# Value product by single heads with high and low parts side by side, and engine orders computed by a list scheduler

## The reference, cut to what matters

```python
s = jnp.einsum("bqhd,bkhd->bhqk", q, k) * scale      # 8 latent heads, then 8 sliding-window heads
s = jnp.where(mask, s, NEG)
p = jax.nn.softmax(s, axis=-1)
o = jnp.einsum("bhqk,bkhd->bqhd", p, v)              # the value product
```

## Time and profile before

| | |
|---|---|
| median of three runs | 1713.6 us |
| profiled execution | 1714.8 us, span 1713.1 us |
| TensorE (PE) busy | 1618.9 us, 95% |
| VectorE | 1127.7 us, 66% |
| GpSimd | 886.8 us, 52% |
| ScalarE | 778.4 us, 45% |
| mean granted TensorE clock | 0.97 of full speed |
| transfers | 285 MB, mean 167 GB/s |

### The profile page before, as it was taken

One profiled execution on the slowest core, in us unless ns is written; L12 is line 12 of the kernel. 1 busy time (PEld: TensorE's weight loads), 2 busy tenths in 40 slices (PEclk: granted clock), 3 DMA queues, 4 the chain that ended last, 5 costly groups with the idle time before them and its releaser, 6 DMA issues. The chain is left out here.

```text
span 1713.1 us, 29386 instructions
## 1 busy us (share of the span) xinstructions
PE 1618.9 (95%) x10253; PEld 1453.7 (85%) x10253; DVE 1127.7 (66%) x1953; ACT 778.4 (45%) x1628; POOL 886.8 (52%) x781
## 2 busy tenths in 40 slices
PE   7999988999997899999999879999999999999997
PEld 6788877888897789888878779999999999778876
DVE  6433344777675667676653696766776766799886
ACT  5221225666776666666542343333333333433354
POOL 1000002665654378686920488777777774444464
PEclk9999996999998999999989989999999999999999
DMA  8366653232322766655576436666666665965532
GB/s 279 117 200 225 219 170 103 59 105 66 84 69 52 199 178 169 176 160 155 168 237 187 157 100 189 179 181 198 205 190 194 189 195 164 355 228 172 177 119 92
DMA packets 218095, 285.35 MB, mean 167 GB/s; under 512 B 35929, under 2 KB 140506, under 8 KB 212780
## 3 DMA queue, kind: packets, MB, share of 16 engines
q1 hardware_dynamic: 217954, 283.53, 54.7%
HBM read 235.92 MB, written 114.67 MB: 205 GB/s over the span
## 5 line engine op out<-in xcount | busy, mean ns | idle before, releaser
L2488 POOL TENSOR_TENSOR lead<-acc,lead 128x512 fp32r<-128x512 f32 x110 | 148.6, 1359 | 104.5 <-ACT lead L2620 104.5
L1114 POOL TENSOR_SCALAR a_pr<-a_pr,a_rden 128x256 f32<-128x256 f32 (+7 forms) x128 | 94.1, 747 | 200.7 <-DVE a_rden L1214 195.9
L819 PE MATMUL zp<-win_h,xT_h 128*128 128x512 f32 (+1 forms) x288 | 113.1, 393 | 3.3 <-DVE acc L668 3.3
L819 PE MATMUL zp<-win_l,xT_h 128*128 128x512 f32 (+1 forms) x288 | 111.8, 388 | 0.0
L2620 ACT CAST lead<-acc 128x512 fp32r<-128x512 f32 x105 | 65.0, 620 | 100.3 <-PE z_ps L3146 58.1
L1155 ACT ACTIVATE a_pr<-a_pr,a_nm 128x256 f32<-128x256 f32 (+7 forms) x128 | 98.5, 772 | 22.3 <-DVE a_nm L1208 21.6
L2678 ACT CAST lead<-d_ring 128x512 fp32r<-128x512 f32 x73 | 45.4, 622 | 129.7 <-PE q_ps L3238 26.3
L1288 PE MATMUL a_o<-a_ph,a_vh 128*128 128x256 f32 x288 | 88.3, 306 | 12.7 <-DVE a_pl L1218 12.5
L819 PE MATMUL zp<-win_h,xT_l 128*128 128x512 f32 (+1 forms) x256 | 99.5, 389 | 0.0
L2559 POOL TENSOR_TENSOR u_op<-d_w,u_op 128x512 fp32r<-128x512 f32 x39 | 54.0, 1387 | 78.8 <-ACT u_op L2690 78.8
L2488 POOL TENSOR_TENSOR u_op<-acc,u_op 128x512 fp32r<-128x512 f32 x44 | 80.3, 1826 | 8.9 <-DVE o_tl L2836 8.9
(11 more groups left out here) (438 smaller groups left out, 5420.1 us busy)
## 6 DMA issues: line engine op xcount, KB each, us to landing
out_s_win_k<-in_state_win_k SPq DMA_DIRECT2D x40, 816.0 KB
out_s_win_v<-in_state_win_v SPq DMA_DIRECT2D x40, 816.0 KB
d_ring<-scratch_s_a SPq DMA_DIRECT2D x106, 256.0 KB, 3.3
acc<-in_state_win_k SPq DMA_DIRECT2D x16, 768.0 KB, 6.0
acc<-in_state_win_v SPq DMA_DIRECT2D x16, 768.0 KB, 5.5
scratch_s_a<-u_us SPq DMA_DIRECT2D x22, 544.0 KB, 6.1
acc<-in_w_gate SPq DMA_DIRECT2D x23, 512.0 KB, 8.9
acc<-in_w_up SPq DMA_DIRECT2D x22, 512.0 KB, 11.6
```

The lines of the kernel that those rows point to most:

```text
L819: last = nc.tensor.matmul(z[:, 0:n], a, b, start=(k == 0 and i == 0), stop=(k == KC - 1 and i == len(terms) - 1))
L1114: nc.gpsimd.tensor_scalar(p, p, self.rden[:, k % 2, h:h + 1], 1.0, ALU.mult, ALU.mult)\
L2488: nc.gpsimd.tensor_tensor(op[n][:, 1, :], src, op[n][:, 0, :].bitcast(F32), ALU.subtract).then_inc(S["lo"], 1)
```

## The change

The diff replaces how the value product is laid out, how its result leaves the bank, how banks are handed out, and how the orders are made.

**Value product.** `vh` and `vl` of a key block now lie in one tile `vv` of four groups of 64 columns: high 0, low 0, low 1, high 1. `ph` and `pl` lie in one tile `pp`, for each block and head the 128 high columns and then the 128 low ones. One matmul for each block and head takes 128 columns of `vv` (one head, high and low) against 256 columns of `pp` (the same head, high and low).

**Output.** In the bank, a head's own 64 rows hold high x high and high x low side by side, the other 64 rows hold low x high in the first 128 columns. VectorE adds the two halves with one `tensor_reduce` for each head, then ScalarE copies the cross terms to free columns of `pr`, then GpSimd adds them. The store waits for GpSimd.

```diff
-        self.vh = [sb(t(f"vh{i}"), [P, PT, 2 * HD], F32R) for i in range(2)]
-        self.vl = [sb(t(f"vl{i}"), [P, PT, 2 * HD], F32R) for i in range(2)]
-        self.ph, self.pl = (sb(t(n), [P, PT, 2, P], F32R) for n in ("ph", "pl"))
+        self.vv = [sb(t(f"vv{i}"), [P, PT, 4 * HD], F32R) for i in range(2)]
+        self.vh = [v[:].rearrange("p j (a c) -> p j a c", a=4)[:, :, 0:4:3] for v in self.vv]
+        self.vl = [v[:].rearrange("p j (a c) -> p j a c", a=4)[:, :, 1:3] for v in self.vv]
+        self.pp = sb(t("pp"), [P, PT, 2, 2, P], F32R)
+        self.ph, self.pl = (self.pp[:, :, :, i] for i in range(2))
+        self.cross = [self.pr[:, 0, i, SEQ - P:] for i in range(2)]
-        self.o_bank = ps(t("o"), [P, 2, P])
+        self.o_bank = ps(t("o"), [P, 2, 2 * P])
...
-            E.append((("value", k), 0.36 * (s + 1)))
+            E.append((("value", k), 0.24 * (s + 1)))
...
         elif what == "store":
-            sp.wait_ge(S["o_a"], n * PT + 4 * f + 4)
-            sp.wait_ge(S["o_d"], n * PT + 4 * f + 4)
+            sp.wait_ge(S["o_sum"], n * PT + 4 * f + 4)
...
     def gpsimd(self, pool, e):
+            v = self.vn[:].rearrange("p j (a c) -> p j a c", a=2)
+            nc.gpsimd.tensor_scalar(vh, v, 1.0, 1.0, ALU.mult, ALU.mult).then_inc(S["v_hi"], 1)
+            nc.gpsimd.tensor_tensor(vl, v, vh.bitcast(F32), ALU.subtract).then_inc(S["v_lo"], 1)
+        elif e[0] == "out":
+            pool.wait_ge(S["o_a"], 2 * k + 2)
+            pool.wait_ge(S["o_d"], 2 * k + 2)
+            nc.gpsimd.tensor_tensor(out, out, self.cross[k % 2], ALU.add).then_inc(S["o_sum"], 1)
...
     def scalar(self, act, e):
-            if s % 4 == 0 and n:
-                act.wait_ge(S[f"o_out{s // 4}"], 16 * n)
-            nc.scalar.copy(self.ot[0:HD, s * P:(s + 1) * P], self.o_bank[0:HD, 0, :]).then_inc(S["o_a"], 1)
+            act.wait_ge(S["o_d"], 2 * k + 2)
+            if k >= 2:
+                act.wait_ge(S["o_sum"], k - 1)
+            for h in range(2):
+                to, of = (slice(x * HD, (x + 1) * HD) for x in (h, 1 - h))
+                nc.scalar.copy(self.cross[k % 2][to], self.o_bank[of, h, 0:P]).then_inc(S["o_a"], 1)
...
     def vector(self, dve, e):
-            nc.vector.tensor_copy(self.ot[HD:P, s * P:(s + 1) * P], self.o_bank[HD:P, 1, :]).then_inc(S["o_d"], 1)
+            for h in range(2):
+                r = slice(h * HD, (h + 1) * HD)
+                nc.vector.tensor_reduce(self.ot[r, s * P:(s + 1) * P], self.o_bank[r, h].rearrange("p (a q) -> p q a", a=2),
+                                        AX.X, ALU.add).then_inc(S["o_d"], 1)
...
     def tensor(self, pe, e):
             if k:
-                pe.wait_ge(S["o_a"], k)
-                pe.wait_ge(S["o_d"], k)
+                pe.wait_ge(S["o_a"], 2 * k)
+                pe.wait_ge(S["o_d"], 2 * k)
-                    for i, (x, y) in enumerate(((vh, self.ph), (vh, self.pl), (vl, self.ph))):
-                        last = nc.tensor.matmul(self.o_bank[:], x[:, kb, :], y[:, kb], start=(kb == 0 and i == 0),
-                                                stop=(kb == s and i == 2))
+                    for h in range(2):
+                        last = nc.tensor.matmul(self.o_bank[:, h], self.vv[n % 2][:, kb, h * P:(h + 1) * P],
+                                                self.pp[:, kb, h].rearrange("p a q -> p (a q)"),
+                                                start=(kb == 0 and h == 0), stop=(kb == s), skip_group_check=True)
```

```diff
+        for u, (e, _) in enumerate(used["tensor"]):
+            self.use[e], self.at[e] = u, placed[e]
+            self.prior[e], holder[placed[e]] = holder[placed[e]], e
...
     def take(self, pe, e):
-        u = self.use[e]
-        if u >= len(self.banks):
-            self.done(pe, self.by[u - len(self.banks)])
+        if self.prior[e]:
+            self.done(pe, self.prior[e])
         return self.bank(e)
...
+    def start(self, part):
+        needs = [(x, lag) for x, lag in self.needs[part] if x in self.busy]
+        if any(x not in self.end for x, _ in needs) or any(x in self.busy and x not in self.end for x in self.gate.get(part, ())):
+            return None
+        at = max([self.clock[part[1]]] + [self.end[x] + HAND[part[1]] + lag for x, lag in needs])
+        if part in self.gate:
+            banks = self.free_banks()
+            return max(at, banks[0][0]) if banks else None
+        return at
...
+    def step(self):
+        best = None
+        for eng in ENGINES:
+            able = []
+            for i in range(2):
+                kinds = set()
+                for x in self.waiting[eng, i]:
+                    if x[1][0] not in kinds:
+                        kinds.add(x[1][0])
+                        at = self.start((i, eng, x[1]))
+                        if at is not None:
+                            able.append((at, x))
+                    if len(kinds) == AHEAD:
+                        break
+            if able:
+                until = max(self.clock[eng], min(at for at, _ in able)) + SLACK
+                at, x = min((c for c in able if c[0] <= until), key=lambda c: self.place[c[1]])
+                if best is None or at < best[0]:
+                    best = at, eng, x
+        at, eng, (i, e) = best
+        if part in self.gate:
+            self.placed[e] = self.free_banks()[0][1]
...
-            run(own, ring, sides, turns_of(weave(sides, ((0, 1), (0.09, 0.97))), LATENT_LATER))
+            run(own, ring, sides, ((0, 1), (0.1, 0.98)))
...
-            run(own, ring, sides, turns_of(weave(sides, ((0, 1), (0.04, 0.97))), DILATED_LATER))
+            run(own, ring, sides, ((0, 1), (0.02, 0.92)))
```

More of the change, by code:

```diff
@@ L910, in take @@
     def take(self, pe, e):
[L912 to L914 removed]
+        if self.prior[e]:
+            self.done(pe, self.prior[e])
         return self.bank(e)
     def bank(self, e):
[L918 removed]
+        return self.banks[self.at[e]]
     def ready(self, eng, e):
@@ L1069, in bank_use, with work @@
         return {"prep": "hd", "score": "d", "turn": "hd"}.get(e[0])
+    def work(self, e):
+        k = e[0]
+        if k in ("load_qk", "load_v", "store"):
+            return {"sync": {"load_qk": (2.2 if e[1] else 1.05, 3.0), "load_v": (0.5, 3.0), "store": (0.4, 2.2)}[k]}
+        if k == "prep":
+            late = self.kind(e[1])
+            return {"tensor": 0.436, "scalar": (0.48, (0.96, 1.92)[e[2]])[late], "vector": (0.62, 1.24)[late]}
+        if k == "swap":
+            return {"scalar": 0.95}
+        if k == "split_v":
+            return {"gpsimd": 3.45}
+        if k == "score":
+            w = self.chunks(e[1] % PT)[e[3]][1]
+            return {"tensor": matmuls((3, 2)[self.kind(e[1] // PT)], w), "vector": (0.35 if e[3] else 0.29) + (w - P) * 0.00104}
+        more = e[1] % PT * P
+        if k == "exp":
+            return {"scalar": 2 * (0.46 + more * 0.000835)}
+        if k == "over":
+            return {"vector": 0.09, "gpsimd": 2 * (0.37 + more * 0.00083)}
+        if k == "turn":
+            m = min(2, e[1] % PT + 1 - 2 * e[2])
+            return {"tensor": 0.218 * m, "scalar": (0.28, 0.48)[m - 1], "vector": (0.35, 0.615)[m - 1]}
+        if k == "value":
+            return {"tensor": matmuls(2 * (e[1] % PT + 1), 2 * P)}
+        return {"vector": 0.75, "scalar": 0.35, "gpsimd": 0.45}
@@ L1760, with __init__, describe, free_banks @@
-DILATED_LATER = {
-    "gpsimd": {(1, "v_split"): -18},
-    "scalar": {(0, "exp"): 3, (0, "prep"): -3, (0, "swap"): 2, (1, "exp"): 4, (1, "fold"): 7,
-        (1, "q_block"): 13},
-    "vector": {(1, "lead_rows"): -3, (0, "out"): -2, (1, "k_turn"): 1, (1, "score"): 1},
-    "tensor": {(0, "prep"): -5, (0, "score"): -1, (0, "turn"): -2, (1, "fold"): 4, (1, "k_turn"): -3,
-        (1, "p_turn"): -2},
-}
+class Turns:
+    def __init__(self, sides, spans, banks):
+        self.sides, self.order = sides, weave(sides, spans)
+        self.place = {x: n for n, x in enumerate(self.order)}
+        self.busy, self.tail, self.needs, self.gate = {}, {}, {}, {}
+        for i, e in self.order:
+            self.describe(i, e)
+        self.end, self.placed = {}, {}
+        self.holder, self.clock = [None] * banks, dict.fromkeys(ENGINES, 0.0)
+        self.turns = {eng: [] for eng in ENGINES}
+        self.waiting = {(eng, i): [x for x in self.order if x[0] == i and (i, eng, x[1]) in self.busy]
+                        for eng in ENGINES for i in range(2)}
+        for _ in range(len(self.busy)):
+            self.step()
+    def describe(self, i, e):
+        work, after = self.sides[i].work(e), self.sides[i].after(e)
+        chain = CHAIN.get(self.sides[i].bank_use(e), ())
+        for eng, cost in work.items():
+            part = (i, eng, e)
+            self.busy[part], self.tail[part] = cost if isinstance(cost, tuple) else (cost, TAIL[eng])
+            self.needs[part] = [(x[:3], x[3] if len(x) > 3 else 0.0) for x in after.get(eng, ())]
+            if eng in chain[1:]:
```

(23 more changed lines are left out.)

197 lines of the change are left out of this document (175 added, 22 removed).

## The result

The changed kernel takes 1671.4 us (median of four, 1666.3 to 1674.5) against 1714.9 us; the ratio is 0.9752, 95% interval 0.9726 to 0.9778. That is 43 us less where 37 were forecast. The total came out near the forecast.

A forecast was written before the change was run, and what follows sets the result against it. It took the attention stages as bound by TensorE's instruction stream: 1714.8 - 34.3 (matmuls) + 9 (stalls) + 3.4 (stage ends) - 14 (orders) = 1678.9, less 1.2 for the median, forecast 1677 us. Range 1660 to 1690 (0.60); 8 in 10: 1651 to 1705.

The forecast's parts named there:

- The count and the price of the matmuls: Value product in both attention stages: 288 fewer matmuls, 576 left, 0.119 us each, 34.3 us less.
- should come back nearly in full: TensorE in the attention stages: work taken out of its stream returns as time, 34.3 us taken, bounds 0 and 34.
- bound by TensorE's instruction stream: Both attention stages: TensorE nearly always has work, busy 220.0 of 225 and 258.5 of 270 us in the dense stretches.
- The emptying: Output bank: two reductions of 0.41 us, copies, then GpSimd's sum; per step VectorE gains 0.53 us, ScalarE 0.26, GpSimd 0.46.
- The 9 us of stalls: Dense stretches: a third of VectorE's extra emptying work shows as new stalls, 9 us, ends 0 and 28.
- Stage ends: Last value product of each attention stage: the store starts 1.7 us later, twice, 3.4 us more.
- 0.2 us for hand-overs: Emptying of the output bank: estimated 0.2 us for passing work between engines, part of the 1.7 us at each stage end.
- The orders, 14 us won: Both attention stages: computed orders and free choice of bank win 14 us of idle time, ends 35 won and 30 lost.
- Moving the spans, priced at nothing: Window side's first steps moved from 0.04 to 0.02: transfers go to the already full start, worth nothing.
- VectorE takes over: Rival, dense stretches: all of VectorE's extra work shows as 28 us of stalls, orders win 10; 1701 us, chance 0.14.
- the chain rival: Slower rival: emptying stands in ScalarE's and VectorE's queues, one late step delays the next, 0.75 us a step; 1731 us, chance 0.09.
- The clock rival: Slower rival: sparser TensorE work brings 14 more clock falls of about 3.5 us, no gain from orders; 1732 us, chance 0.02.

The follow-up runs named there:

- the two with other loads: Changed kernel with the second window pair's loads issued after step 3, not 0: 1664.9 us; the same with the planner told they need step 3: 1668.4 us.
- measured costs: Changed kernel with the planner's emptying costs set to the trace's, VectorE 0.87 us (was 0.75) and ScalarE 0.54 (was 0.35): 1688.8 us, ratio to before 0.9848.
- rotation: Changed kernel with the planner made to hand out banks in rotation, which gives a new plan: 1707.4 us, ratio to before 0.9959.
- old spans: Changed kernel with the decode side's spans and three early places as before, which gives a new plan: 1715.8 us, ratio to before 1.0002.
- the product-only kernel: Kernel before with the new value product and its emptying, but old fixed orders and banks in rotation: 1720.9 us, ratio to before 1.0045.
- with two terms: Kernel before with the third value matmul of each block (low values x high probabilities) left out, orders held: 1703.6 us, ratio to before 0.9931.
- the one-step kernel: Changed kernel with the window side's span in the second stage ending at 0.93, not 0.92, a new plan: 1687.1 us, ratio to before 0.9883.
- the kernel with the later sum: New product and emptying in the old orders, with GpSimd's output sum 8 places later in its order: 1724.6 us, ratio to before 1.0079.

## Why the prediction was right in its total and wrong in its terms

Chance has a part in the total. Orders computed from nearly the same numbers put the same kernel anywhere between 1665 and 1716 us, and five of the seven tried lie in the forecast's range of 1660 to 1690. What is off in the terms, one by one:

- **The count and the price of the matmuls** held: 576, 0.12 us apart. That their 34.3 us "should come back nearly in full" did not. With nothing else changed 12 us came back. The step that failed is the first one, "bound by TensorE's instruction stream": I saw that up to 0.16 us of gap hides behind each drawn end and still took 220.0 of 225 us busy as full. In the held order 8 us of the shortened work came back as visible idle time and up to 8 at the lower clock. That the shorter product only brings a consumer nearer to its producer is my reading of it; no listed wait is long enough to show it. Nor is it shown that the 34 us came through in the changed kernel.
- **The emptying.** Durations held (0.42 us a reduction, 0.26 a copy, 0.46 a sum). The 9 us of stalls is mis-sized and not one number: some 19 us (13 to 26) with the stage ends in the old orders, nothing that can be taken back in the changed plan, and 36 us when its VectorE part is doubled there.
- **Stage ends** were worth 3.4 us in the sum. The last value matmul of the first stage starts at 518.1, the next stage at 521.32 us, 3.2 us against 2.4. At the second end it takes 3.4 against 1.5. That is 2.7 us in all. The prediction's 0.2 us for hand-overs is met: 0.08 us from the reductions to the copies, 0.08 to the sum, 0.02 to the store. The rows of the first end:

```profile
517.65 0.74 PE L1367 MATMUL a_o<-a_pp,a_vv 128*128 128x256 f32 x4
518.42 0.88 DVE L1304 TENSOR_REDUCE a_ot<-a_o 64x128 f32<-64x256 f32 x2 [0.83 <-PE a_o L1367]
519.38 0.54 ACT L1246 COPY a_pr<-a_o 64x128 f32<-64x128 f32 x2 [1.63 <-PE a_o L1367]
520.00 0.45 POOL L1197 TENSOR_TENSOR a_ot<-a_ot,a_pr 128x128 f32<-128x128 f32 x1 [6.13 <-ACT a_pr L1246]
520.47 0.33 SPq L1165 DMA_DIRECT2D scratch_s_o<-a_ot  x1
...
521.32 1.09 PE L1323 MATMUL l_bank<-ident_sb,a_kn 128*128 128x128 f32 x4 [2.93 <-PEq L2422]
```

- **The orders, 14 us won,** with ends of 35 won and 30 lost. This is the term that decided the result. The sum left the starts out of it, and the first stage's start alone gave some 8 us. Over seven plans of the same program parts (the changed kernel, the two with other loads, measured costs, one step of a span, rotation, old spans) the ratio runs from 0.970 to 1.000, 51 us. The change's plan is among the best of these. I took the orders for a correction of 14 us to the product's gain; which plan one has moves the time by more than the product's 34 us. Moving the spans, priced at nothing, is part of it: with the old spans the whole gain is gone. What the product gives under one and the same computed order was not measured.
- **The rivals.** "VectorE takes over" did not happen at 84%. The dearer emptying did cost some 19 us in the product-only kernel, as the chain rival had it for the old orders; but TensorE's listed waits for low parts grow by 5 us only (5.8 and 12.9 against 4.7 and 8.8 with two terms), so its mechanism, a queue that one late step stops, is not shown. The clock rival had 2%. It counts one fall of the clock in 495 us of dense work; the trace has a second, short one at 642 us, behind the mean of 0.99 in the second stretch. The clock goes with the larger part of what separates the second stage of the one-step kernel from the changed one's (13 of 16 us), and the kernel with the later sum misses 21 us more by it than the kernel before (48 against 27).
- **Still open:** what the free choice of bank is worth. Rotation could only be tried with another plan, and plans alone differ by more. Open too is how much the lower clock costs by itself: it comes where TensorE starts fewer matmuls. In the one-step kernel TensorE waits 1.3 and 0.5 us just before the clock falls at 593.6 us. So it follows waits there, and then lengthens what comes behind; no run held the order and changed only the clock. And how much of the 43 us is the product's stays open.

## What to carry to other kernels

Don't count work taken out of the fullest engine at its full price: here 34 us gave 12 (7 to 17) with the order held. Try the edit alone in the held order first, since one line (a term left out) told more here than all rows of busy time. Where orders come from a planner, treat one plan as one draw: move its free numbers by a step and time several before crediting an edit with 20 us, and compare parts only with the order held. Read the stages and not only the total: the rest behind them moved by 13 us with no edit there. A waiting engine with a large total (179 us here) need not be on the path: moving that wait changed nothing.

## What the runs showed of the hardware

- The granted clock in the midst of a stage differs with the order of the same instructions: 0.57 as a mean over 15 us (670 to 685) in the one-step kernel, 1.00 in the changed kernel, with both stages made of the same events. The mean clocks of whole executions agree: 0.968 to 0.972 in four of the one, 0.973 to 0.977 in four of the other.
- VectorE's sum of two strided 64x128 views of a bank takes 0.423 us, about as much as a subtraction over 256 dense columns (0.415): against that row the stride of 128 between the two addends costs no more than 0.01 us.
- GpSimd's 128x128 sum takes 0.457 us in the median of 64, at any place of the stages (0.444 to 0.487).
